# Ranking 50 instead of 256 pairs in a router's second top-16, on VectorE beside a TensorE stream

## What is computed

```python
q = (h @ w_q).reshape(B, S, 8, 2, 128)
sc = einsum('bshpd,phnd->bshpn', q, keys)          # 8 heads, 2 key sets, 128 scores each
v1, i1 = top_k(sc[..., 0, :], 16)                  # first round
v2, i2 = top_k(sc[..., 1, :], 16)
cand = v1[..., :, None] + v2[..., None, :]         # 16 x 16 = 256 pairs
cidx = i1[..., :, None] * 128 + i2[..., None, :]
best, pos = top_k(cand.reshape(..., 256), 16)      # second round
idx = take_along_axis(cidx, pos)
gates = softmax(best)
...
act = gelu(einsum('tkd,td->tk', u[idx], h))        # u, v: 16384 x 1024
out = einsum('tk,tkd->td', gates * act, v[idx])
```

## Time and profile before

| | |
|---|---|
| median of 3 runs | 1378.35 us (1378.18 to 1378.45) |
| the profiled execution | 1378.15 us |
| its span in the profile | 1376.1 us |
| PE busy, of the span | 99% |
| DVE busy, of the span | 75% |
| granted TensorE clock, mean of the span | 0.998 of full speed |

### The profile page before, as it was taken

How to read it: one execution, slowest core, us unless ns; L and a number is a source line. 1 busy time by engine, 2 the same in 40 slices (tenths; PEclk the granted TensorE clock), 3 DMA queues, 4 the chain that set the end, 5 groups by cost and what they waited for, 6 DMA issues and landing times.

```text
span 1376.1 us, 26736 instructions
## 1 busy us (share of the span) xinstructions
PE 1357.4 (99%) x10948; PEld 1290.1 (94%) x10949; DVE 1036.9 (75%) x1848; ACT 737.2 (54%) x1078; POOL 292.8 (21%) x176
## 2 busy tenths in 40 slices
PE   9999999999999999999999999999999999999997
PEld 7989989999999999999999999999998798899986
DVE  5556575593987899989999888887887664777744
ACT  5674645545464444444444456555677554655543
POOL 6000000388874222220000033320132000100001
PEclk9999999999999999999999999999999999999999
DMA  7443355455569777775555589986443543555552
GB/s 248 140 136 123 128 195 215 141 197 199 197 221 333 280 242 247 247 258 181 186 185 185 194 323 349 350 308 237 149 146 107 182 154 116 176 184 185 185 190 99
DMA packets 76585, 279.26 MB, mean 203 GB/s; under 512 B 8496, under 2 KB 8752, under 8 KB 76208
## 3 DMA queue, kind: packets, MB, share of 16 engines
q1 hardware_dynamic: 67104, 243.73, 51.5%
q0 software_dynamic: 9216, 33.56, 6.5%
q10 hardware_dynamic: 144, 0.26, 0.1%
HBM read 276.47 MB, written 1.05 MB: 202 GB/s over the span
## 4 chain that ended last, share of the span: by engine, by line
PE 89%; ACT 4%; DVE 4%; POOL 1%; issue 1%; DMA 0%; POOLq 0%; SPq 0%; DVEq 0%
PE bank L478 88%; ACT A L1232 2%; PE bank L487 1%; DVE wlo L1828 1%; ACT whi L1232 1%; DVE A L1828 1%; POOL wlo L2780 1%; ACT L1232 1%; DMA xres<-in_x 0%; DVE xres L1828 0%; DVE A L1824 0%; ACT hT L1232 0%; DVE small L2576 0%; DVE A L1825 0%; DVE small L1828 0%
## 5 line engine op out<-in xcount | busy, mean ns | idle before, releaser
L478 PE MATMUL bank<-hT,whi 128*128 128x224 f32 (+2 forms) x5148 | 1008.7, 293 | 2.6 <-DVE wlo L1828 1.7
L478 PEld LDWEIGHTS bank<-hT,whi 128*128 128x128 f32 x5148 | 811.4, 190 | 18.8 <-DVE wlo L1828 2.5
L478 PE MATMUL bank<-hT,wlo 128*128 128x224 f32 (+1 forms) x2952 | 810.8, 275 | 0.0
L1232 ACT ACTIVATE whi<-raw 128x1024 fp32r<-128x1024 f32 (+1 forms) x450 | 473.1, 1054 | 352.2 <-PE bank L478 344.5
L1828 DVE TENSOR_TENSOR wlo<-raw,whi 128x1024 fp32r<-128x1024 f32 (+1 forms) x386 | 472.9, 1226 | 226.3 <-ACT whi L1232 226.0
L478 PEld LDWEIGHTS bank<-hT,wlo 128*128 128x128 f32 x2952 | 562.6, 191 | 0.0
L1232 ACT ACTIVATE A<-bank 128x512 f32<-128x512 f32 (+4 forms) x170 | 90.2, 537 | 213.1 <-PE bank L478 203.5
L2780 POOL TENSOR_TENSOR wlo<-raw,whi 128x1024 fp32r<-128x1024 f32 x62 | 148.6, 2414 | 111.9 <-ACT whi L1232 109.4
L2796 POOL DMA_INDIRECT A<-in_v,small x32 | 50.5, 1578 | 288.1 <-DVE A L1824 174.1
L2796 POOL DMA_INDIRECT A<-in_utab,small x32 | 54.5, 1704 | 132.5 <-DVE A L1831 131.0
L2786 POOL TENSOR_TENSOR small<-small 128x1 f32<-128x1 f32 x14 | 8.3, 594 | 339.8 <-DVE small L1825 336.7
(11 more groups left out here) (183 smaller groups left out, 1327.4 us busy)
## 6 DMA issues: line engine op xcount, KB each, us to landing
raw<-in_u SPq DMA_DIRECT2D x128, 512.0 KB, 3.3
raw<-in_v SPq DMA_DIRECT2D x128, 512.0 KB, 3.6
raw<-in_w_up SPq DMA_DIRECT2D x44, 512.0 KB, 3.2
raw<-in_w_down SPq DMA_DIRECT2D x22, 512.0 KB, 3.3
raw<-in_w_in_t SPq DMA_DIRECT2D x17, 512.0 KB, 4.0
raw<-in_w_in_g SPq DMA_DIRECT2D x16, 512.0 KB, 3.2
raw<-in_w_out SPq DMA_DIRECT2D x16, 512.0 KB, 3.6
raw<-in_w_pq SPq DMA_DIRECT2D x16, 512.0 KB, 3.6
```

The costliest lines, as they stand in the source:

```text
L478: return e.matmul(o, l, r, start=st, stop=sp_, skip_group_check=True)
L1232: return e.activation(o, i, func, **kw)
```

## The change

Among 16 sorted scores of one set and 16 of the other, the pair (i, j) can be among the best 16 sums only if (i + 1)(j + 1) is at most 16. There are 50 such pairs: 16 for i = 0, 8 for i = 1, then 5, 4, 3, 2, 2, 2 and eight times 1.

```diff
+BEST_OF = [16 // (i + 1) for i in range(16)]
+NBEST = sum(BEST_OF)
+BEST_BLOCKS = [(0, 1, 16), (1, 1, 8), (2, 1, 5), (3, 1, 4), (4, 1, 3), (5, 3, 2), (8, 8, 1)]
+WIDE = (2, 2)
...
                 v2p = t3(banks[7][:, 16:16 + P], 8)
+                pay = t3(candw[:, 8 * NBEST:8 * NBEST + P], 8)
                 own(e.tensor_copy(v2p, vv[:, :, 1, :]))
                 again()
-                own(tt(t4(cand, 8, 16), vv[:, :, 0, :].unsqueeze(3).to_broadcast(shape),
-                       v2p.unsqueeze(2).to_broadcast(shape), ALU.add))
+                own(e.tensor_copy(pay[:, :, 0:1], iv[:, :, 0, 0:1]))
+                own(tt(pay[:, :, 1:16], iv[:, :, 0, 1:16], iv[:, :, 0, 0:15], ALU.subtract))
+                at = 0
+                c50, w50 = (t3(z[:, 0:8 * NBEST], 8) for z in (cand, candw))
+                for i, n, w in BEST_BLOCKS:
+                    shape = [P, 8, n, w]
+                    own(tt(c50[:, :, at:at + n * w].rearrange("p h (n w) -> p h n w", n=n),
+                           vv[:, :, 0, i:i + n].unsqueeze(3).to_broadcast(shape),
+                           v2p[:, :, 0:w].unsqueeze(2).to_broadcast(shape), ALU.add))
+                    at += n * w
+                again()
+                own(tt(pay, pay, banks[7][:, 160:176].unsqueeze(1).to_broadcast([P, 8, 16]), ALU.add))
                 yield
...
-                yield from top16(t3(cand, 8), t3(candw, 8), bv, pu, 8, 4)
-                pall = posu[:, 0:128].bitcast(U32)
-                again()
-                ts(posu[:, 128:256].bitcast(U32), pall, 4, None, ALU.logical_shift_right)
-                own(ts(posu[:, 256:384].bitcast(U32), pall, 15, None, ALU.bitwise_and))
+                yield from top16(c50, w50, bv, pu, 8, 8)
                 again()
-                own(e.tensor_copy(posf, posu[:, 128:384].bitcast(U32)))
+                own(e.tensor_copy(posf[:, 0:P], posu[:, 0:P].bitcast(U32)))
...
                 for q in range(2):
                     ps = t3(posf[:, q * P:(q + 1) * P], 8)
+                    ref = (banks[7][:, 144:160], banks[7][:, 0:16])[q].unsqueeze(1).unsqueeze(1).to_broadcast(part)
+                    worth = iv[:, :, 1, :] if q else pay
+                    dst = sel_i[1] if q else scw[:, 400:528]
+                    for h in range(2):
+                        again()
+                        for g in (2 * h, 2 * h + 1):
+                            own(tt(t4(banks[g][:, :], 2, 16), ps[:, 2 * g:2 * g + 2, :].unsqueeze(3).to_broadcast(part),
+                                   ref, ALU.is_equal if q else ALU.is_ge))
+                        again()
+                        for g in (2 * h, 2 * h + 1):
+                            own(tt(t4(oh2[:, g * 512:(g + 1) * 512], 2, 16), t4(banks[g][:, :], 2, 16),
+                                   worth[:, 2 * g:2 * g + 2, :].unsqueeze(2).to_broadcast(part), ALU.mult))
+                            if g == 2 * h:
+                                yield
+                        again()
+                        own(e.tensor_reduce(t3(dst[:, 64 * h:64 * h + 64], 4),
+                                            t4(oh2[:, 1024 * h:1024 * h + 1024], 4, 16), AX, ALU.add))
+                        yield
+                    if q == 0:
+                        pi = posu[:, P:2 * P].bitcast(U32)
+                        again()
+                        own(e.tensor_copy(pi, dst))
+                        again()
+                        own(ts(posu[:, 2 * P:3 * P].bitcast(U32), pi, 8, None, ALU.logical_shift_right))
+                        again()
+                        own(e.tensor_copy(posf[:, P:2 * P], posu[:, 2 * P:3 * P].bitcast(U32)))
+                        again()
+                        own(stt(sel_i[0], posf[:, P:2 * P], -256.0, dst, ALU.mult, ALU.add))
+                        again()
+                        own(tt(posf[:, P:2 * P], posf[:, 0:P], posf[:, P:2 * P], ALU.subtract))
+                        yield
```

More of the change, by code:

```diff
@@ L77 @@
     ("ident", 128), ("g_mix", 8), ("g_ffn", 8), ("g_mix2", 8), ("g_x2", 8), ("g_mem2", 8), ("g_ffn2", 8),
-    ("iota", 128), ("iota16", 16),
+    ("iota", 128), ("iota16", 16), ("first16", 16), ("steps16", 16),
     ("cfw", 66), ("cfb", 22), ("pick", NG),
@@ L172 @@
 own_act own_dve own_pool zeros x_sq hi_half lo_half lo_first f_xd f_act hd_mask
-pk_idx pk_rep pk_used pk_act v_tile v_b v_sum v_tr x_g
+pk_idx pk_rep pk_used pk_act v_tile v_b v_sum v_tr u_low u_sum x_g
 """.split()
@@ L386, in cut, with u_part, is_wide @@
             return both_cuts(n)[:, part, :]
+        def u_part(n):
+            return og[:, 2 * TD * (n % 2):2 * TD * (n % 2 + 1)].bitcast(F32)
+        def is_wide(n):
+            return WIDE[0] <= n < WIDE[1]
         v_banks = (0, 1, 2, 3, 5, 6, 4, 4)
@@ L628, in lin_T, with wide @@
                         after(u)
+                    side.step(steps[(i + 1) % len(steps)])
+            def wide(u0, u1, steps):
+                both = t4(hT[:, :], 2, KD)
+                for u in range(u0, u1):
+                    i = BASE["u"] + u
+                    wv = two(unit(i), KD)
+                    b = 4 + (u - 1) % 3
+                    use(b)
+                    for k in range(KD):
+                        mm(banks[b][:, 0:2 * TD], wv[0][:, k, :], both[:, :, k, NG:T], k == 0, False)
+                        ins = mm(banks[b][:, 0:TD], wv[1][:, k, :], both[:, 0, k, NG:T], False, k == KD - 1)
+                        if 2 * (k + 1) == KD:
+                            mid.step()
+                    ins.then_inc(s["w"], 1)
+                    free[b] = (s["u_sum"], u - WIDE[0] + 1)
+                    pair[0] += u % 2
                     side.step(steps[(i + 1) % len(steps)])
@@ L1092, in pe_program @@
             side.lists[0] += [routing(0), routing(1)]
-            lin_T(BASE["u"], 62, hTv, KD, steps=U1_STEPS, c0=NG)
+            lin_T(BASE["u"], WIDE[0], hTv, KD, steps=U1_STEPS, c0=NG)
+            wide(*WIDE, U1_STEPS)
+            lin_T(BASE["u"] + WIDE[1], 62 - WIDE[1], hTv, KD, steps=U1_STEPS, c0=NG)
             side.drain()
@@ L1403, in routing @@
             def routing(b):
-                for _ in range(21):
+                for _ in range(19):
                     yield
@@ L1408, in routing @@
                 yield
-                for _ in range(8):
+                for _ in range(10):
                     yield
@@ L1681, in act_program, with take_low @@
             side.lists[0] += [routing(0), routing(1)]
-            lin_T(BASE["u"], 62, gelu(0), rep_h, steps=U1_STEPS)
+            def take_low(n):
+                if n - 2 >= WIDE[0]:
+                    e.wait_ge(s["u_sum"], n - 1 - WIDE[0])
+                e.wait_ge(s["w"], BASE["u"] + n + 1)
+                act(u_part(n), banks[4 + (n - 1) % 3][:, TD:2 * TD], ACT.Copy).then_inc(s["u_low"], 1)
+            for u in range(62):
+                hi(BASE["u"] + u + 2)
+                if is_wide(u - 1):
+                    take_low(u - 1)
+                if u % 2 and is_wide(u - 3):
+                    e.wait_ge(s["u_sum"], u - 1 - WIDE[0])
+                    z = acts[:, u - 3:u - 1, :]
+                    act(z, z, ACT.Gelu).then_inc(s["ev_act"], 1)
+                    pair[0] += 1
+                if u % 2 and not is_wide(u):
+                    e.wait_ge(s["w"], BASE["u"] + u + 1)
+                    gelu(u - 1)(0, t3(banks[4 + pair[0] % 3][:, :], 2))
+                    pair[0] += 1
+                rep_h(u)
+                side.step(U1_STEPS[(BASE["u"] + u + 1) % len(U1_STEPS)])
             side.drain()
@@ L2143, in routing @@
                 tt(t3(bex, 8), bv, bv[:, :, 0:1].to_broadcast([P, 8, 16]), ALU.subtract).then_inc(s["rt_dve"], 1)
                 yield
+                part = [P, 2, 16, 16]
                 for q in range(2):
                     ps = t3(posf[:, q * P:(q + 1) * P], 8)
[L2147 to L2159, removed]
+                    ref = (banks[7][:, 144:160], banks[7][:, 0:16])[q].unsqueeze(1).unsqueeze(1).to_broadcast(part)
@@ L2665, in dve_program, with add_low @@
             own(e.tensor_copy(banks[7][:, 0:16], K_("iota16")))
+            own(e.tensor_copy(banks[7][:, 144:176], keep[:, KOFF["first16"][0]:KOFF["first16"][0] + 32]))
             own(e.tensor_copy(t3(iota_b[:, :], P), K_("iota").unsqueeze(2).to_broadcast([P, P, 2])))
             side.lists[0] += [routing(0), routing(1)]
-            lin_T(BASE["u"], 62, before=pick_u, steps=U1_STEPS)
+            def add_low(u):
+                n = u - 1
+                if is_wide(n):
+                    e.wait_ge(s["u_low"], n - WIDE[0] + 1)
+                    tt(acts[:, n, :], banks[4 + (n - 1) % 3][:, 0:TD], u_part(n), ALU.add).then_inc(s["u_sum"], 1)
+                pick_u(u)
+            lin_T(BASE["u"], 62, before=add_low, steps=U1_STEPS)
             side.drain()
@@ L2987, in shape_constants @@
         "iota": np.broadcast_to(np.arange(P), (P, P)), "iota16": np.broadcast_to(np.arange(16), (P, 16)),
```

(2 more changed lines are left out.)

1 line of the change is left out of this document (removed).

## The result

| | before | after |
|---|---|---|
| median, us | 1378.26 (1377.99 to 1378.6, 6 runs) | 1385.23 (1385.21 to 1385.56, 6 runs) |
| ratio to before | | 1.0051, 95% interval 1.0038 to 1.0064 |
| span of the profiled execution, us | 1376.1 | 1383.2 |
| DVE busy, us | 1036.9 | 1041.2 |

What follows compares the result with a forecast made beforehand. PE was taken to bound the kernel, so DVE's saving of some 18 us counted nothing; only the PE wait at unit 53 changed, 0.46 to 0.4 us, giving a median of 1378.3 us, range 1377.6 to 1379.6.

Steps and rivals of the forecast that it cites:

- The step that failed: In routing, the copy to bank 7 and the wider keep come where DVE waits for scores: no cost.
- the rivals: Product clear of the gather (0.25); port decides, slower (0.13); DVE's time is PE's, or change ineffective (0.02, fast side).
- PE's instructions are the same: Units computed in another form are an empty range, so that part of the change is worth nothing.
- A beat other than 5.36 us: Sign against the whole reasoning: two units of u taking PE something other than 5.36 us.
- Ranking: DVE's MAX8, replaces and finds in each routing block, over 50 instead of 256: saves 9.0 us a block.
- Waits for POOL: Added SBUF-only DVE operations in routing wait for running POOL instructions: about 10 us more in block 1.
- DVE idle for over 20 us before the first transposes: Sign between the routing blocks: block 0's saving of 8.8 us adds to DVE's 17.6 us of idle time.
- The PE wait at unit 53: PE waiting for POOL's last correction of the stage: 0 to 0.8 us in place of 0.46, 0.4 kept.
- Rival 2: Block 1's row product, delayed by port waits, holds ACT and PE: up to 3.6 us lost, 1382.0 us; chance 0.13.

Runs made afterwards that it cites:

- e1: The kernel before with the tile keep 32 columns (128 bytes a partition) wider and nothing else changed: 1384.77 us, ratio 1.0047.
- e17: The changed kernel with its two new tables in a tile at the end of SBUF and unit 53's correction on DVE instead of POOL: 1377.77 us, ratio 0.9997.
- e2: The changed kernel with its two new tables in a tile at the end of SBUF, other tiles at their old addresses: 1378.55 us, ratio 1.0003.
- e16: The kernel before with keep 48 columns (192 bytes) wider, distance from whi0 to hT 160 modulo 256: 1380.01 us, single run.
- e13: The changed kernel with keep another 24 columns wider, tiles placed as in the kernel before with keep 56 wider: 1369.68 us, ratio 0.9942.
- e18: The changed kernel with keep another 24 columns wider and unit 53's correction on DVE instead of POOL: 1370.21 us, ratio 0.9936.
- e14: The changed kernel with keep another 24 columns wider and REP_AT 46 instead of 51, row product five units earlier: 1369.71 us, ratio 0.9937.

## Why the prediction was wrong

**The step that failed** is "The copy of 32 columns to bank 7 and the wider `keep` lie in front of it, where DVE waits for the scores, and cost nothing." I counted the transfer and the copy. I did not count that a wider tile moves every tile behind it. e1 shows what that alone costs: 6.6 of the 7.0 us, by a slower pace of PE (5.76 us for two units in `w_pq` instead of 5.68); over the units of `u` it adds no delay. None of the rivals had it, and "PE's instructions are the same" was true of all but their addresses.

**The scope was wrong too.** "A beat other than 5.36 us would make the whole reasoning wrong" looked for the right sign in the one stage where it could not show: two units of `u` next to each other took 5.36 us in the trace of every kernel here. A look at `w_pq` would have found 5.76.

**Ranking.** Predicted 0.113, 0.178 and 0.180 us over 50. Replaces and finds came at 0.18 from start to start; MAX8 takes 0.125. The straight line through two lengths came close.

**Waits for POOL.** Predicted about 10 us more in block 1, and the row product at 399.3. It came at 398.9 on the scale of before, 9.6 behind the 389.3 without waits. The rule of the Trainium skill ("SBUF — State Buffer", "Who interferes with whom") carried this term, and the trace agrees: copy, subtraction, shift and cast all show rows of 2.0 to 2.5 us (the shift, 2.31 us, in block 0). DVE's busy time rose by 4.3 us, though its work fell. But I had expected "DVE idle for over 20 us before the first transposes", and it was idle for 17.6 us as before. Block 0 paid its waits as well, and I had charged them to block 1 alone. It cost nothing.

**The PE wait at unit 53.** Predicted 0 to 0.8 us in place of 0.46, with 0.4 kept; it was 0.87, just past the end. e17 shows that it hung on this correction standing behind the gather on POOL's queue. With the places held (e2) the sum was 1378.55, inside the range and 0.25 over the forecast.

**Rival 2**, the port deciding, didn't happen: the product came before its point of 401.7, and no PE wait for DVE grew.

## What to carry to other kernels

A constant added to an early tile moves all later tiles. In a kernel bound by TensorE compare the addresses of what PE reads before and after, and look at its pace in stages that the change doesn't touch. Put new tables behind the rest, or pad so that the distance between weights and moving operand stays; and when all is tuned, sweep that padding over 256 bytes in steps of 32, since here its best value gave back 11 us and the changed routing cost 0.4. Time each value several times: at the best one the six runs lay between 1367.26 and 1373.75 us. Making an engine faster that nobody waits for gains nothing; and where the new version adds operations on SBUF alone beside a busy POOL, even that engine's own gain can be lost to waiting.

## What the runs showed of the hardware

The pace of PE at full granted clock (0.998 to 0.999 in these runs) changed with the distance between the tiles it reads weights from and the tile it moves: from 5.44 to 5.76 us for the same 48 products of 256 columns in `w_pq` by moving `keep`'s end, and 5.81 with `whi` and `wlo` shifted against each other. Steps of 256 and 512 bytes gave the pace of before (5.68), and so did moving all tiles together by 128. The distance alone doesn't fix it: at distance 192 the same products took 5.44 or 5.65 us, and in e16 (160) 5.70 in `w_pq` and 5.76 in `w_up`. A conflict between PE's two streams of reads would look like this, but no run shows the mechanism. Why one place goes at two paces stays open as well.

A copy of 8 numbers a partition took 2.04 us on DVE when POOL held a correction, and POOL's first gather took 1.97 to 1.99 us where DVE was at an operation with two SBUF inputs meanwhile (the row product in the changed kernel, e2 and e13, unit 53's correction in e17 and e18), against 1.21 before and in e14, where DVE was idle for nearly all of it. The second gather took 1.76 us in the changed kernel, beside a DVE correction, and 0.94 in e17 and e18, beside operations with a PSUM operand.
